# Scaling the attention probabilities on ScalarE, head by head, with transposes that follow each head

## What is computed

```python
sc = jnp.einsum('bqhd,bkhd->bhqk', q_blk, k).astype(jnp.float32)
sc = jnp.where(causal[None, None], sc, -jnp.inf)
p = jax.nn.softmax(sc, axis=-1).astype(v.dtype)
return jnp.einsum('bhqk,bkhd->bqhd', p, v)
...
p = jax.nn.softmax(jnp.concatenate([sc, sink], axis=-1), axis=-1)[..., :-1].astype(v.dtype)
out = jnp.einsum('bnkgqs,bnskd->bnqkgd', p, vv)
```

## Time and profile before

| what | value |
|---|---|
| median of three runs | 1969.0 us (1964.46 to 1974.37) |
| the profiled execution, its own time | 1965.62 us |
| its span, first to last instruction | 1963.9 us |
| TensorE busy (matmuls) | 1868.7 us, 95% |
| VectorE busy | 830.4 us, 42% |
| ScalarE busy | 635.5 us, 32% |
| GpSimd busy | 53.1 us, 3% |
| mean granted TensorE clock | 0.991 |

### The profile page before, as it was taken

How to read it: one execution, slowest core, us unless ns; L and a number is a source line. 1 busy time by engine, 2 the same in 40 slices (tenths; PEclk the granted TensorE clock), 3 DMA queues, 4 the chain that set the end, 5 groups by cost and what they waited for, 6 DMA issues and landing times. The chain is left out here.

```text
span 1963.9 us, 36108 instructions
## 1 busy us (share of the span) xinstructions
PE 1868.7 (95%) x15682; PEld 1281.4 (65%) x15694; DVE 830.4 (42%) x1689; ACT 635.5 (32%) x1211; POOL 53.1 (3%) x58
## 2 busy tenths in 40 slices
PE   7899999999999998999999989999899999999997
PEld 6889998889997887744444434378776444444343
DVE  5767777767775575411111111155734111111113
ACT  4565555565554341311111111143313111111112
POOL 0500000400000000000000000000000000000000
PEclk9999999999999999999999999999999999999999
DMA  7235554245542235699999999633339999999993
GB/s 286 103 140 190 190 194 168 87 151 192 182 163 79 89 98 214 278 427 427 425 428 426 427 426 428 296 123 110 139 117 425 426 427 427 426 426 428 426 427 162
DMA packets 54241, 540.18 MB, mean 275 GB/s; under 512 B 8608, under 2 KB 9536, under 8 KB 16704
## 3 DMA queue, kind: packets, MB, share of 16 engines
q1 hardware_dynamic: 54080, 537.83, 67.7%
HBM read 536.76 MB, written 1.05 MB: 274 GB/s over the span
## 5 line engine op out<-in xcount | busy, mean ns | idle before, releaser
L2865 PE MATMUL experts_psG<-places_gu,experts_xc 128*64 128x512 f32 x1344 | 298.9, 596 | 9.2 <-DMA places_gu<-in_moe_up 8.0
L511 DVE TENSOR_TENSOR ring_low<-ring_raw,ring_high 128x1024 fp32r<-128x1024 f32 x180 | 222.2, 1245 | 100.6 <-ACT ring_high L505 100.5
L2865 PEld LDWEIGHTS experts_psG<-places_gu,experts_xc 128*64 128x64 f32 x1344 | 97.0, 137 | 204.1 <-issue 187.1
L644 PE MATMUL ffn_ps<-first_x_split,ring_high 128*128 128x512 f32 x616 | 220.6, 396 | 0.3
L2795 DVE SCALAR_TENSOR_TENSOR experts_yc_low<-experts_psD,experts_slot_gate,experts_yc_high 128x512 fp32r<-128x512 f32 x64 | 48.0, 750 | 388.3 <-ACT experts_yc_high L2829 388.3
L505 ACT ACTIVATE ring_high<-ring_raw 128x1024 fp32r<-128x1024 f32 x180 | 186.8, 1051 | 70.8 <-PE ffn_ps L646 30.7
L645 PE MATMUL ffn_ps<-first_x_split,ring_low 128*128 128x256 f32 x704 | 183.4, 281 | 0.0
L2785 DVE TENSOR_TENSOR experts_sig<-experts_sig,experts_psG 128x256 f32<-128x256 f32 x64 | 26.9, 421 | 357.2 <-ACT experts_sig L2817 357.2
L2865 PE MATMUL experts_psG<-weights_gu,experts_xc 128*64 128x512 f32 x704 | 156.0, 593 | 4.3 <-DMA weights_gu<-in_moe_up 4.3
L2817 ACT ACTIVATE experts_sig<-experts_psG 128x256 f32<-128x256 f32 x64 | 24.5, 383 | 413.2 <-PE experts_psG L2865 413.2
L645 PEld LDWEIGHTS ffn_ps<-first_x_split,ring_low 128*128 128x128 f32 x704 | 132.1, 188 | 7.1
(11 more groups left out here) (520 smaller groups left out, 3268.6 us busy)
## 6 DMA issues: line engine op xcount, KB each, us to landing
ring_raw<-in_w SPq DMA_DIRECT2D x90, 1024.0 KB, 4.8
places_gu<-in_moe_gate SPq DMA_DIRECT2D x42, 2048.0 KB, 28.5
places_gu<-in_moe_up SPq DMA_DIRECT2D x42, 2048.0 KB, 29.9
places_d<-in_moe_down SPq DMA_DIRECT2D x32, 2048.0 KB, 30.1
weights_gu<-in_moe_gate SPq DMA_DIRECT2D x22, 2048.0 KB, 27.3
weights_gu<-in_moe_up SPq DMA_DIRECT2D x22, 2048.0 KB, 28.8
weights_d<-in_moe_down SPq DMA_DIRECT2D x16, 2048.0 KB, 26.0
experts_d_more<-in_moe_down SPq DMA_DIRECT2D x16, 2048.0 KB, 28.8
```

The source lines that it names most:

```text
L511: dve.tensor_tensor(self.low[:, n % AHEAD], self.raw_half(n), self.high[:, n % AHEAD], ALU.subtract)\
L644: pe.matmul(out, w[0][:, kk], f.both[:, :, kk], start=kk == 0, stop=False)
L2865: ins = pe.matmul(out, xc[:, kk], wgu[gu[0]][:, kk, :, j * S:(j + 1) * S], start=kk == 0, stop=kk == DT - 1)
```

## The change

In `normalise(u)` VectorE keeps the sum and the reciprocal and no longer multiplies. A new `normalise(u)` in ScalarE's list waits for the reciprocal (`rden_ready`) and scales each head with its own Copy whose scale operand is the head's column of `rden`. Each head's Copy raises `probs_ready`, and TensorE's transposes wait for their own head only.

```diff
@@ vector
-                    ch.link(dve.reciprocal(rden[:, u % 2], den[:, u % 2]))
-                    dve.tensor_tensor(pr[:, :, 0:n], pr[:, :, 0:n], bc(rden[:, u % 2], n, 2), ALU.mult)\
-                        .then_inc(probs_ready, 1)
+                    dve.reciprocal(rden[:, u % 2], den[:, u % 2]).then_inc(rden_ready, 1)
@@ scalar
+                def normalise(u):
+                    n, pr = P * (units[u][1] + 1), prob[:, u % 2]
+                    act.wait_ge(rden_ready, u + 1)
+                    for h in range(HEADS):
+                        act.activation(pr[:, h, 0:n], pr[:, h, 0:n], ACT.Copy, scale=rden[:, u % 2, h:h + 1])\
+                            .then_inc(probs_ready, 1)
...
                 exps(0)
                 ring.round(act, base + 12)
+                normalise(0)
                 exps(1)
                 ring.round(act, base + 13)
                 copy_probs(0)
+                normalise(1)
                 ring.round(act, base + 14)
                 copy_y(0)
                 copy_probs(1)
                 exps(2)
                 ring.round(act, base + 15)
                 copy_y(1)
+                normalise(2)
                 exps(3)
...
                 square(1, pool_copied, 2)
                 ring.round(act, base + 18)
+                normalise(3)
                 copy_y(2)
                 copy_probs(3)
@@ tensor
                 def transpose(u):
                     blk = units[u][1]
-                    pe.wait_ge(probs_ready, u + 1)
                     for h in range(HEADS):
+                        pe.wait_ge(probs_ready, HEADS * u + h + 1)
                         for kb in range(blk + 1):
```

More of the change, by code:

```diff
@@ L696, in stage_mix1 @@
          q_done, k_done, v_done, q_copied, kv_copied, vT_done, vT_copied, scores_done, scores_read, max_ready,
-         exp_done, probs_ready, transposed, probT_ready, attended, y_copied, pool_ready, pool_mixed, pool_copied,
+         exp_done, rden_ready, probs_ready, transposed, probT_ready, attended, y_copied, pool_ready, pool_mixed, pool_copied,
          conv_ready, g_squares, g_sums, g_ln, g_rstd_ready, g_normed, g_rounded, g_split, out_done,
@@ L701, in stage_mix1 @@
              "q_done k_done v_done q_copied kv_copied vT_done vT_copied scores_done scores_read max_ready "
-             "exp_done probs_ready transposed probT_ready attended y_copied pool_ready pool_mixed pool_copied "
+             "exp_done rden_ready probs_ready transposed probT_ready attended y_copied pool_ready pool_mixed pool_copied "
              "conv_ready g_squares g_sums g_ln g_rstd_ready g_normed g_rounded g_split out_done added").split()]
```

## The result

The changed kernel takes 1972.88 us (median of 7 runs, 1970.59 to 1974.73), the kernel before in the same session 1966.79 us (7 runs, 1963.61 to 1974.37). The ratio is 1.003, with a 95% interval of 1.0015 to 1.0044: about 6 us slower. A second measurement gave 1971.24 (11 runs) against 1967.67 (23 runs), ratio 1.0023, interval 1.0012 to 1.0033, about 4.5 us. Both intervals exclude no change, though the loss is only a quarter of a per cent.

A forecast was written before the change was run, and what follows sets the result against it. TensorE, busy for 95% of the span, bounds the kernel, so only its idle or slowed time counts. Waiting of 2 x 2.6 us plus 1.6 for a clock fall gives +6.8: 1969.0 + 6.8 = 1975.8 us, range 1967.5 to 1981.5.

The forecast's parts named there:

- the prices: ScalarE's four Copies per unit: 1.69 us at 256 columns, 1.33 at 128; 0.65 us a layer more by durations alone.
- unit 0: First unit's scaling: TensorE loses about 0.3 us, absorbed by later idle time; unit 1's exponentials start 1.5 us late.
- unit 1: Second unit's scaling ends at 64.1 to 65.75; TensorE's loss is -0.3 to +1.3 us, taken as +1.3.
- the two hindered rows: VectorE's rest of a tile (2.06 us) and 128x4 addition (0.99), slowed by GpSimd before unit 1's reciprocal: the upper bound.
- what is queued behind unit 1's scaling: Tile 14's round delays soften(2) by 0.3 to 2.8 us; without slack, group(0) comes 0 to 2.2 late, taken as +2.1.
- unit 3: Scaling behind group(0)'s roundings, square(1) and a round starts at 85.65 to 87.85; group(1) 0.8 to 3.0 us later, taken +2.6.
- The clock: Longer idle time before unit 3's transposes brings one further fall of TensorE's clock in the two layers, 1.6 us.
- The sum: Whole kernel: 2 x 2.6 + 1.6 = 6.8 us slower, bounds 0 and 10.8; chance of this forecast 0.55.
- a change of length beyond the two mixers: Sign against the prediction: work outside the two layers' mixers changes its length.
- Nothing moves: Rival: GpSimd is out of VectorE's way more often, lower bounds hold, 0 to 2 us, 1970; chance 0.17.
- Slower by the clock: Rival: three or more further clock falls at units 3 and 1, 10 us or more, 1980; chance 0.20.
- Overlap: Rival: transposes run beside scalings, unit 3's scaling starts before 84.0, up to 2 us a layer faster, 1965; chance 0.08.

The follow-up runs named there:

- e8: Changed kernel with only units 0 and 2 scaled on VectorE again; 1970.3 us in one run.
- e1: Changed kernel with only unit 3 scaled on VectorE again; 1964.24 us in one run.
- e2: Changed kernel with unit 3's scaling moved ahead of group(0)'s roundings in ScalarE's list; 1965.29 us over 12 runs, ratio to before 0.9989.
- e3: Changed kernel with the round of tile 14 put ahead of unit 1's scaling in ScalarE's list; 1963.46 us in one run.
- e5: Changed kernel with eight matmuls whose results nobody reads put on TensorE before unit 3's transposes; 1972.61 us in one run.
- e9: Kernel before with square(1) alone moved ahead of group(0)'s roundings in ScalarE's list; 1964.34 us over 12 runs, ratio to before 0.998.
- e6: Changed kernel with units 0 and 2 on VectorE, unit 1's scaling behind tile 14's round, unit 3's ahead of group(0)'s roundings; 1962.51 us, ratio to before 0.998.
- e4: Changed kernel with the transposes of a unit waiting for all four heads; 1976.07 us in one run.
- e7: e6 with square(1) also moved up in ScalarE's list, ahead of unit 3's scaling; 1959.55 us over 6 runs, ratio to before 0.9966.

## Why the prediction was right, and where its sizes were off

The forecast was +6.8 us and the two measurements say about +6 and +4.5; the sign, the mechanism and the range hold. It came out closer than its terms deserve: three of them erred, partly in opposite directions, and only 2.3 to 3.7 us of the loss are there at the start of the second block, where the forecast had all of it. That the total comes out near 6.8 is luck in part.

**Right: the prices.** Four Copies of 256 columns take 1.69 and 1.71 us (1.69 forecast); four of 128 take 1.28 (1.33, from an Exp). The rule in "ScalarE: Activation LUTs", Rules for kernel authors, of the Trainium skill, that multiplications belong on VectorE, holds here by price for the narrow units (0.69 us against 1.28) and not for the wide ones, where VectorE needed 1.93 and 2.08.

**Right: unit 0.** The exponentials of unit 1 begin at 57.68 (57.7 forecast), `attend(0)` at 61.33 (61.3), and TensorE lost nothing against before by it, as forecast. It is not free for unit 1, though: with unit 0 back on VectorE (e8) the scaling of unit 1 starts 60.88 - 48.39 = 12.49 us after the stretch's start and not 63.34 - 49.35 = 13.99.

**Between the bounds: unit 1.** The reciprocal is done at 63.31 (62.4 to 64.05). One of the two hindered rows came back as such: the addition of 128x4 elements takes 0.99 us again, and the rest ahead of it 1.35 where I had taken 2.06. The scaling ends at 63.34 + 1.71 = 65.05 (64.1 to 65.75). TensorE is through 0.7 us later than before; I had taken +1.3.

**Mis-sized: what is queued behind unit 1's scaling.** The start was right: the rest of tile 14 begins at 66.03 (64.7 to 66.3) and `soften(2)` at 67.17, 1.5 us late. But I let that lateness run through undiminished, "with no slack". It did not. The rest of tile 14 took 1.23 us and not 2.06, which those 1.5 us contain already. Behind it two more rows of before had been slow, and came back as short ones: the last step of `soften(2)` and the rest of tile 15, which ran beside GpSimd's addition. In the order VectorE, GpSimd, before:

```profile
67.06 0.64 DVE L790 TENSOR_SCALAR mix_nmx<-mix_mx 128x4 f32<-128x4 f32 x1
...
70.37 2.17 DVE L511 TENSOR_TENSOR ring_low<-ring_raw,ring_high 128x1024 fp32r<-128x1024 f32 x1 [1.94 <-ACT ring_high L505]
```

```profile
70.17 1.29 POOL L744 TENSOR_TENSOR mix_pooled<-mix_pooled,mix_up 128x512 f32<-128x512 f32 x1
```

and in the changed kernel:

```profile
68.61 0.17 DVE L790 TENSOR_SCALAR mix_nmx<-mix_mx 128x4 f32<-128x4 f32 x1
```

```profile
68.73 1.28 POOL L744 TENSOR_TENSOR mix_pooled<-mix_pooled,mix_up 128x512 f32<-128x512 f32 x1
```

The addition ended at 70.01, ahead of the rest at 71.44, which took 1.22 us. So from `soften(2)` on 0.47 and 0.95 us came back, besides the 0.6 to 0.7 us of the multiply that the prediction had counted: 2.1 in all, which turns 1.5 us late into 0.6 early. `square(0)` starts at 77.35 (77.96 before), and `group(0)` 28.95 us after the stretch's start where it had been 29.33: 0.4 us early, not 2.1 late. The step of the prediction that failed is "I take +2.1, since I took the upper bound above", and with it the line that the 0.73 us before `group(0)` would be at least as long; that wait is gone.

**Right in mechanism, mis-sized: unit 3.** Because of that line 807 starts at 81.90, ahead of the 82.65 to 84.85 that I gave its predecessor, line 809. It stands right behind the reciprocal, as forecast. But from its start to the end of `square(1)` it took 84.28 + 0.61 - 81.90 = 2.99 us, where I had taken the 2.05 of before: the line itself ran for 2.02 us and not for 1.09. So the scaling starts at 85.75, at the lower bound of 85.65 to 87.85, and still behind 84.0, the point named for the overlap to win. The wait is ended by ScalarE and is 3.56 us, the 0.89 before `group(1)` is gone, `group(1)` starts 38.71 - 37.45 = 1.26 us later (+0.8 to +3.0; I took +2.6), and `project(15)` behind it 1.8 later, where I had named 2 to 3 as the sign (TensorE's first row of it is at 89.41, before at 87.53). e1 shows that without unit 3's part there is no loss, and e2 that an earlier place on ScalarE removes it. But e3 removes it as well with the scaling left in place, so the round behind unit 1's scaling, which the prediction had as the start of its lateness, has its part in it.

**The clock: right that it falls, wrong where and how often.** I took one further fall in the two layers. The changed kernel has one at unit 3 in each, worth 0.9 us (e5), and 2.3 in layer 1 of its second profile, where it lasted longer (46.22 against 43.96). The kernel before has falls of its own, and a price of 1.6 for each was wrong: at `group(1)` a fall costs 1.56, at unit 1 it costs 0.13 (43.13 against 43.00), since the waits behind it swallow it (there is none before `group(0)` in that layer, where layer 0 has 0.73 us, and unit 3's was 1.03 and not 1.60); e9 shows the same, 41.98 us with it and 41.97 without.

**The sum.** Waiting is 2 x 1.0 us (e5 against the first profile of before), and in the second pair of profiles the starts of unit 3's transposes and of `group(1)` are the same. With the clock, the first routing matmul of the second block begins 816.5 - 812.8 = 3.7 us later in the first pair of profiles and 815.4 - 813.1 = 2.3 later in the second; my 6.8 was to be all there by then. The rest of the medians' 4.5 to 6 us lies behind it and is not settled. From that matmul to the last of its kind in the next layer it took 669.6 us before and 672.9 after, then 666.8 and 669.7 in the second pair, but 672.3 and 672.0 in e8 and e6 and 669.1 and 670.3 in e3 and e9: 6 us of scatter that no edit orders. I had written that a change of length beyond the two mixers would speak against me; one pair of profiles cannot tell it, and it stays open whether the change has any part in it.

**The rivals.** "Nothing moves" (0 to 2 us) is excluded by both intervals. "Slower by the clock" (10 us or more) did not come in the changed kernel; e4 comes near to it, at 9 us over before, with falls at two units in both layers. "Overlap" needs unit 3's scaling to start before 84.0 and got 85.75; in e2 it started at 80.73, and e2 is faster than before.

## What to carry to other kernels

When work is moved from one engine to another, the order of the receiving engine's list can matter more than the duration of the work: the same four Copies lose or win time by where they stand, and by whether a round that another engine needs stands behind them (e3). Look for the stretch in which the receiving engine waits, just where the operand becomes ready, and put the work there; small independent instructions (a square, a round) can be moved into such waits as well, with or without the larger change. A lateness is not carried through a chain undiminished when some links were long only because another engine was in their way: ask of each slow row of before whether it will still be slow at its new time.

## What the runs showed of the hardware that was not expected

- The granted clock of the kernel before fell at `group(1)` in both layers in one execution and in neither in another. In layer 0 the idle times ahead of it were the same, 1.60 and 0.89 us. What decides it is not settled. A fall in one layer's attention cost between nothing (e9) and 2.3 us (second profile of the changed kernel), by how long it lasts and what waits follow.
- Filling one gap (e5) took the fall from that place; the one run, at 1972.61 us, was no faster than the changed kernel. Filling the gaps with useful work (e7) left the attention of both layers at full clock and won.
- VectorE's line 809 of before, two operations of 128x256 elements with three operands, took 1.09 us; as line 807 of the changed kernel it took 2.02. It ran there while GpSimd worked on line 747 (80.84 to 83.03); in the kernel before, the multiply of 2.08 us stood at that place (GpSimd's 81.46 to 83.64). Taking the multiply away from VectorE so won about half of its length: the next in its list was as slow in the same place. Over all thirteen profiles and both layers this instruction, the first of its line in a layer, took 2.02 to 2.06 us in the 18 cases in which it ran beside GpSimd's line 747, and 1.09 us in the 8 in which line 747 had ended; e1, which puts the multiply back ahead of it, brings the 1.09 back (83.26, behind line 747's end at 82.25). No run took GpSimd's work away, so the cause is read from timelines and not tested by itself.
